# GpSimd's overflow steps dealt over seven turns of the expert loop, and a last stage whose first tile VectorE sums

## The reference, cut to what matters

```
order = jnp.argsort(e_flat)                  # tokens sorted by expert
xs = h2[slot_tok].reshape(n_blocks, MOE_BLOCK, d)
def expert_block(args):
    xb, e = args
    return (jax.nn.silu(xb @ w_gate[e]) * (xb @ w_up[e])) @ w_down[e]
ys = ys * slot_gate[:, None]
moe = jnp.zeros((n, d)).at[slot_tok].add(ys)
x = x + gt2 * moe
return rmsnorm(x, g_final)
```

## Time and profile before

| | us |
|---|---|
| median of 3 runs | 1537.36 |
| lowest, highest | 1535.84, 1541.0 |
| the profiled execution, its own time | 1537.67 |
| its span, first to last instruction | 1535.6 |
| TensorE busy in it | 1376.1 (90%) |
| VectorE busy | 931.7 (61%) |
| ScalarE busy | 679.1 (44%) |
| GpSimd busy | 283.9 (18%) |

### The profile page before, as it was taken

The page is one execution under the profiler, slowest core; times in us unless marked ns, Lnnn a source line. Parts: engine busy times, 40 slices in busy tenths (PEclk is TensorE's granted clock), DMA queues, the critical chain, the costliest instruction groups (busy, mean ns, idle before and its releaser), DMA issues. The chain is left out here.

```text
span 1535.6 us, 16837 instructions
## 1 busy us (share of the span) xinstructions
PE 1376.1 (90%) x6490; PEld 971.6 (63%) x6490; DVE 931.7 (61%) x1077; ACT 679.1 (44%) x772; POOL 283.9 (18%) x208
## 2 busy tenths in 40 slices
PE   1699999899999999989996647999999999999955
PEld 1555566456565665674554536888888888888832
DVE  8431230355555554654336564998898998988828
ACT  3500111123333332441111544877787878787713
POOL 0000010311111213210000693222222222222100
PEclk9899999899999999999997778999999999999968
DMA  9393235422222322343112574999999999999734
GB/s 358 103 305 113 68 108 168 134 61 79 70 82 70 88 74 66 92 143 124 69 55 83 189 300 147 382 395 382 383 369 392 379 390 382 388 381 385 270 147 200
DMA packets 101269, 321.47 MB, mean 209 GB/s; under 512 B 12140, under 2 KB 57284, under 8 KB 76613
## 3 DMA queue, kind: packets, MB, share of 16 engines
q1 hardware_dynamic: 89669, 296.25, 53.1%
q0 software_dynamic: 9216, 16.80, 2.9%
q10 hardware_dynamic: 2304, 7.34, 1.2%
HBM read 308.81 MB, written 28.31 MB: 220 GB/s over the span
## 5 line engine op out<-in xcount | busy, mean ns | idle before, releaser
L1630 DVE TENSOR_TENSOR w_low<-raw,w_high 128x2048 fp32r<-128x2048 f32 x128 | 291.7, 2300 | 38.6 <-ACT w_high L1570 36.0
L1570 ACT ACTIVATE w_high<-raw 128x2048 fp32r<-128x2048 f32 x128 | 240.9, 1908 | 15.8 <-PEq L981 15.8
L827 PE MATMUL p_j<-arena,raw 128*128 128x512 f32 (+1 forms) x448 | 184.3, 558 | 11.9 <-DVE raw L744 9.4
L1630 DVE TENSOR_TENSOR w_low<-arena,w_high 128x2048 fp32r<-128x2048 f32 x64 | 146.4, 2290 | 32.0 <-ACT w_high L1570 32.0
L827 PEld LDWEIGHTS p_j<-arena,raw 128*128 128x128 f32 x448 | 82.6, 192 | 86.4 <-issue 81.8
L1546 POOL DMA_INDIRECT y_rows<-arena,row x32 | 46.5, 1455 | 423.0 <-ACT arena L1591 422.7
L1570 ACT ACTIVATE w_high<-arena 128x2048 fp32r<-128x2048 f32 x64 | 122.3, 1912 | 3.3 <-DMA arena<-in_w_down 3.3
L449 PE MATMUL p_v<-wv,arena 128*128 128x384 f32 x320 | 105.5, 493 | 7.7 <-DMA wv<-in_w_in 7.7
L1504 PE MATMUL p_g<-w_high,x_high 128*128 128x512 f32 x256 | 103.6, 405 | 4.6 <-DVE x_low L1635 4.6
L1504 PE MATMUL p_y<-w_high,h_high 128*128 128x512 f32 x256 | 100.3, 392 | 3.4 <-issue 3.4
L761 DVE CUSTOM_DVE_ANT_0 prob<-p_s,table 128x640 f32<-128x640 f32 x96 | 75.2, 821 | 46.3 <-PE p_s L865 46.1
(11 more groups left out here) (286 smaller groups left out, 2504.9 us busy)
## 6 DMA issues: line engine op xcount, KB each, us to landing
raw<-in_w_gate SPq DMA_DIRECT2D x64, 1024.0 KB, 8.0
raw<-in_w_up SPq DMA_DIRECT2D x64, 1024.0 KB, 7.4
arena<-in_w_down SPq DMA_DIRECT2D x64, 1024.0 KB, 7.6
wa<-in_w_ada SPq DMA_DIRECT2D x24, 1024.0 KB, 6.4
table<-in_rpb SPq DMA_DIRECT2D x96, 192.0 KB
yy<-y_rows SPq DMA_DIRECT2D x8, 1024.0 KB, 12.7
raw<-in_w_in SPq DMA_DIRECT2D x12, 512.0 KB, 3.8
raw<-v_rows SPq DMA_DIRECT2D x96, 64.0 KB
```

What stands on the lines that cost most here:

```text
L827: last = pe.matmul(dst[:, 0:cols.stop - cols.start], wqk[:, k, w, :], s.ht[:, k, cols], start=(k == 0), stop=(k == KD - 1))
L1570: act.activation(x.high[i % SPLITS][:], x.raw[j][:, :], ACT.Copy).then_inc(high_ok, 1)
L1630: dve.tensor_tensor(x.low[i % SPLITS][:], x.raw[j][:, :], x.high[i % SPLITS][:], ALU.subtract).then_inc(low_ok, 1)
```

## The change

`build` is cut into seven methods with the same 80 steps in the same order: `count`, `add_up`, `owners`, `starts`, `turns`, `blocks`, `places`. They are called in turns 1 to 7 of GpSimd's loop, one each. In `finish`, tile 0 gets no diagonals and no TensorE products: VectorE makes two `scalar_tensor_tensor` and two adds. The `gain` row, its product and its copy go; ScalarE issues a DMA that reads `g_final` for all 128 partitions into `gains`.

```diff
@@ main_experts, gpsimd
+            steps = Counter(pool, over_ready)
             pool.wait_ge(c_in, 16)
             for n in range(NE):
                 if n + 2 < NE:
                     pool.wait_ge(x_turned, n + 1)
                     gather(pool, a, s, n + 2)
-                if n == 0:
-                    over.build(pool, Counter(pool, over_ready), s)
                 if n >= 1:
                     scatter(n - 1)
+                if n == 1:
+                    over.count(pool, steps)
+                if n == 2:
+                    over.add_up(pool, steps)
+                if n == 3:
+                    over.owners(pool, steps, s)
+                if n == 4:
+                    over.starts(pool, steps)
+                if n == 5:
+                    over.turns(pool, steps)
+                if n == 6:
+                    over.blocks(pool, steps)
+                if n == 7:
+                    over.places(pool, steps)
             scatter(NE - 1)
@@ finish, sync
-                sp.dma_start(gain[:], a.g_final).then_inc(g_in, 16)
                 for i in range(NT):
@@ finish, gpsimd
-                pool.memset(onerow[:], 1.0).then_inc(consts, 1)
                 pool.memset(epsb[:], EPS).then_inc(consts, 1)
@@ finish, tensor
-                pe.wait_ge(consts, 2)
-                pe.wait_ge(g_in, 16)
-                for h in range(2):
-                    last = pe.matmul(p_n[:, h, :], onerow[:], gain[:, h * 512:(h + 1) * 512], start=True, stop=True)
-                last.then_inc(spread, 1)
-                for i in range(NT):
+                for i in range(1, NT):
                     pe.wait_ge(y_in[i], 16)
-                    pe.wait_ge(diags, 2 * (i + 1))
-                    if i >= 2:
+                    pe.wait_ge(diags, 2 * i)
+                    if i >= 3:
                         pe.wait_ge(added, 2 * (i - 2) + 1)
@@ finish, scalar
-                act.wait_ge(spread, 2)
-                act.activation(halves(gains[:]), p_n[:], ACT.Copy).then_inc(spread_ok, 1)
-                act.wait_ge(consts, 2)
+                act.dma_start(gains[:], a.g_final.to_broadcast([P, D])).then_inc(g_in, 16)
+                act.wait_ge(consts, 1)
@@ finish, vector
+                def add_first():
+                    x1 = s.x1[:, 0, :]
+                    dve.wait_ge(y_in[0], 16)
+                    dve.wait_ge(spread_ok, 1)
+                    for k in range(2):
+                        c.step(dve.scalar_tensor_tensor(gated[k][:], yy[0][:, k, :], s.gates[:, k, 0:1], gate2[:], ALU.mult, ALU.mult))
+                    for k in range(2):
+                        dve.tensor_tensor(x1, x1, gated[k][:], ALU.add).then_inc(added, 1)
+                        dve.wait_ge(added, k + 1)
@@ scale(i)
                     if i == 0:
-                        dve.wait_ge(spread_ok, 2)
+                        dve.wait_ge(g_in, 16)
@@ order of VectorE
-                for i in range(NT):
+                for i in range(1, NT):
                     for k in range(2):
                         ...
                 for i in range(0, NT, 2):
-                    add(i)
+                    if i == 0:
+                        add_first()
+                    else:
+                        add(i)
                     add(i + 1)
```

More of the change, by code:

```diff
@@ L1402, in __init__, with halve, passed, count @@
         self.wide = free
-    def build(self, pool, c, s):
-        U, T = 2 * NT, N // CAP - 1
-        tt, ts = pool.tensor_tensor, pool.tensor_scalar
[L1410 to L1426, removed]
+    def halve(self, c, tt, dst, x, n):
+        while n > 2:
+            n //= 2
+            c.step(tt(x[:, :, 0:n], x[:, :, 0:n], x[:, :, n:2 * n], ALU.add))
+        c.step(tt(dst, x[:, :, 0], x[:, :, 1], ALU.add))
+    def passed(self, c, tt, ts, dst, x, n, compare):
+        flag = self.wide[:, 0:n]
+        c.step(ts(dst, x, float(CAP), None, compare))
+        for i in range(2, N // CAP):
+            c.step(ts(flag, x, float(CAP * i), None, compare))
+            c.step(tt(dst, dst, flag, ALU.add))
+    def count(self, pool, c):
+        tt, ts = pool.tensor_tensor, pool.tensor_scalar
+        self.passed(c, tt, ts, self.over, self.total, NE, ALU.is_gt)
+    def add_up(self, pool, c):
+        tt = pool.tensor_tensor
         now, other = self.sums
@@ L1433, in build, with owners @@
         c.step(tt(self.first, now, self.over, ALU.subtract))
+        self.upto, self.spent = now, other
+    def owners(self, pool, c, s):
+        tt, ts, now, other = pool.tensor_tensor, pool.tensor_scalar, self.upto, self.spent
         ends = self.wide[0:1, 0:OVB * NE].rearrange("p (b e) -> p b e", b=OVB)
@@ L1438, in build @@
         c.step(ts(ends, ends, 0.0, None, ALU.is_le))
-        halve(other[0:1, 0:OVB], ends, NE)
+        self.halve(c, tt, other[0:1, 0:OVB], ends, NE)
         c.step(ts(other[0:1, 0:OVB], other[0:1, 0:OVB], float(NE - 1), None, ALU.min))
@@ L1442, in build, with starts, turns, blocks @@
         c.step(pool.tensor_copy(s.blocks[:, OVB:OVB + 1], now[0:1, NE - 1:NE]))
+    def starts(self, pool, c):
+        U, tt = 2 * NT, pool.tensor_tensor
         pick = self.wide[:, 0:U * NE].rearrange("p (u e) -> p u e", u=U)
         c.step(tt(pick, self.one_e.rearrange("p (u e) -> p u e", u=U), self.first.unsqueeze(1).to_broadcast([P, U, NE]), ALU.mult))
-        halve(self.start, pick, NE)
-        passed(self.turn, self.rk, U, ALU.is_ge)
+        self.halve(c, tt, self.start, pick, NE)
+    def turns(self, pool, c):
+        U, tt, ts = 2 * NT, pool.tensor_tensor, pool.tensor_scalar
+        self.passed(c, tt, ts, self.turn, self.rk, U, ALU.is_ge)
         c.step(ts(self.rest, self.turn, -float(CAP), None, ALU.mult))
         c.step(tt(self.rest, self.rest, self.rk, ALU.add))
+    def blocks(self, pool, c):
+        U, tt, ts = 2 * NT, pool.tensor_tensor, pool.tensor_scalar
         c.step(tt(self.start, self.start, self.turn, ALU.add))
@@ L1461, in build, with places @@
             c.step(tt(self.code[:, :, d, :], hit, self.digits[:, U * d:U * (d + 1)].unsqueeze(2).to_broadcast([P, U, OVB]), ALU.mult))
+    def places(self, pool, c):
+        U, ts = 2 * NT, pool.tensor_scalar
         for u in range(U):
@@ L1853, in finish @@
         yy = [t.sb(f"yy{b}", [P, 2, D]) for b in range(NT)]
-        diag = t.sb("diag", [P, NT, 2, P])
+        diag = t.sb("diag", [P, NT - 1, 2, P])
         gated = [t.sb(f"gated{b}", [P, D]) for b in range(2)]
-        gain = t.sb("gain", [1, D])
         gains, gate2 = t.sb("gains", [P, D]), t.sb("gate2_rows", [P, D])
-        onerow, epsb = t.sb("onerow6", [1, P]), t.sb("epsb6", [P, 1])
+        epsb = t.sb("epsb6", [P, 1])
         ss, root, rstd, tmp = (t.sb(n, [P, NT]) for n in ("ss6", "root6", "rstd6", "tmp6"))
         p_s = [t.ps(f"p_s6{b}", [P, 2, 512]) for b in range(2)]
-        p_g, p_n = t.ps("p_g6", [P, 2, 512]), t.ps("p_n6", [P, 2, 512])
+        p_g = t.ps("p_g6", [P, 2, 512])
         y_in = [t.sem(f"y_in{b}") for b in range(NT)]
@@ L1902, in _ @@
                         for k in range(2):
-                            last = pe.matmul(p_s[i % 2][:, h, :], diag[:, i, k, :], yy[i][:, k, h * 512:(h + 1) * 512], start=(k == 0), stop=(k == 1))
+                            last = pe.matmul(p_s[i % 2][:, h, :], diag[:, i - 1, k, :], yy[i][:, k, h * 512:(h + 1) * 512], start=(k == 0), stop=(k == 1))
                     last.then_inc(gathered, 1)
@@ L1922, in _ @@
                 c = s.chain.on(dve)
+                def add_first():
[7 more added lines that the diff above has]
+                        dve.wait_ge(added, k + 1)
                 def add(i):
-                    dve.wait_ge(gathered, i + 1)
-                    if i == 0:
-                        dve.wait_ge(spread_ok, 1)
+                    dve.wait_ge(gathered, i)
                     x1, g = s.x1[:, i, :], gated[i % 2]
@@ L1942, in scale @@
                         dve.scalar_tensor_tensor(x1, x1, rstd[:, n:n + 1], gains[:], ALU.mult, ALU.mult).then_inc(scaled, 1)
-                for i in range(NT):
+                for i in range(1, NT):
                     for k in range(2):
-                        dve.tensor_scalar(diag[:, i, k, :], s.ident[:], s.gates[:, k, i:i + 1], None, ALU.mult).then_inc(diags, 1)
+                        dve.tensor_scalar(diag[:, i - 1, k, :], s.ident[:], s.gates[:, k, i:i + 1], None, ALU.mult).then_inc(diags, 1)
                 for i in range(0, NT, 2):
-                    add(i)
+                    if i == 0:
+                        add_first()
+                    else:
+                        add(i)
                     add(i + 1)
```

## The result

The changed kernel takes 1571.18 us (median of 4 runs, 1569.43 to 1574.87) against 1538.11 us, a ratio of 1.0217 (95% interval 1.0191 to 1.0243). That is 2.2% slower, 4 us above the forecast of 1567 and inside its range. The profiled execution took 1572.16 us, its span is 1570.2 us, 34.6 more than before.

What follows compares the result with a forecast made beforehand. TensorE was taken to bound the expert loop at 17.75 us a turn, with one 32.49 us hole. Removed stall -34.3, new waits +56.3, clock +8.4 and last stage -1.3 gave +29.1 us: forecast 1567 us, range 1552 to 1583.

Steps and rivals of the forecast that it cites:

- The removed stall: Expert loop: TensorE's wait for the gather of expert 3 goes, with its clock loss, -34.3 us.
- The order in GpSimd's list: Expert loop: each batch stands between a scatter and the next gather, making four TensorE waits, 56.3 us in sum.
- the short batches: Expert loop: add_up, starts and blocks cost nothing, as each runs during the stall in front of it.
- G: Expert loop: moment when TensorE has finished `gate_up(n, 1)` and wants `turn_x(n + 1)`; the next comes 17.75 us later.
- clock: After each of four stalls TensorE's clock must come back: 2.1 us each, 8.4 in all.
- The landing: Late gathers behind count, owners and turns land 8.0 us after they start; the one behind places takes 5.0.
- Two batches: Owners (10 steps) last until G + 22.6, gather at 23.4; turns (15 steps) until G + 21.5, gather at 22.3.
- On the port: Gather issue beside line 1630 taken as slow, 2.44 us against 1.14; by the skill's page the sum would be 3.9 lower.
- Delays TensorE almost one for one: Expert loop: whatever is put between a scatter and the gather behind it delays TensorE by nearly its own length.
- The 0.7 us between landing and need: Expert loop: a normal gather lands at G + 17.0 and is wanted at G + 17.75, taken as its slack.
- The last stage: `finish`: TensorE sums three tiles instead of four, so tile 3's sum is ready earlier: -1.3 us (-2.6 to +0.4).
- the sign that the fourth tile would start some 1 us earlier: Last stage: the fourth tile's line 1929 should start 1 us or so earlier, relative to the stage's start.

Runs made afterwards that it cites:

- split: Changed kernel, scatters one turn later, places dealt by four over turns 7 to 10; four last-stage variants: 1505.14, 1502.09, 1499.87 and 1499.98 us.
- later: Changed kernel with every scatter one turn later in GpSimd's list, same batches in the same turns: 1519.03 us, ratio 0.9886 to before.
- ahead: Changed kernel with each batch ahead of its turn's scatter instead of behind it: 1525.02 us, ratio 0.9940 to before.
- dose1: Kernel before, with one useless GpSimd step added between scatter and gather in each of turns 8 to 28: 1537.00 us, ratio 1.0003.
- dose4: Kernel before, with four useless GpSimd steps added between scatter and gather in each of turns 8 to 28: 1567.78 us, ratio 1.0192.
- fin_only: Kernel before with only the last stage (`finish`) of the change, overflow steps as before: 1538.04 us, ratio 1.0016.

## Why the prediction was right

**The removed stall** was predicted at 34.3 us and is gone: in the changed kernel turn 2 takes 17.74 us with no wait, and the four `split` kernels, in which nothing takes its place, come out 33 to 38 us faster. From the transposes of expert 2 to those of expert 31 their traces have 514.9 us each, the kernel before 549.3: 34.4 us.

**The order in GpSimd's list** was the right thing to read, and `later` and `ahead` show it. The holes stand where they were predicted, before experts 4, 6, 8 and 10, and the short batches were covered.

| before expert | batch | gather issued at G + | landing | wait | clock |
|---|---|---|---|---|---|
| 4 | count | 20.8, measured 20.8 | 8.0, 10.2 | 11.1, 13.1 | 2.1, 1.5 |
| 6 | owners | 23.4, 21.3 | 8.0, 9.0 | 13.6, 12.5 | 2.1, 2.3 |
| 8 | turns | 22.3, 20.6 | 8.0, 10.4 | 12.6, 13.1 | 2.1, 2.3 |
| 10 | places | 31.7, 31.5 | 5.0, 4.2 | 19.0, 17.9 | 2.1, 1.8 |

The first number is the predicted one. The waits sum to 56.5 against 56.3, the clock to 7.9 against 8.4. That the sum is this close is partly luck: two terms were off and cancel. **The landing was sized too small**, 8.0 where 9.0 to 10.4 was measured. I took the gather at 856 us (7.4) as the nearest row, but its issue of 2.29 us began before the weights flowed. From the end of the issue the three landings take 6.7 to 7.3 us; the rest is the issue itself, 2.4 to 3.0 us beside line 1630. **Two batches were sized too long**, owners by 2.1 and turns by 1.7 us: more steps found VectorE between line-1630 instructions than I had placed there (of the 15 of turns ten took 0.22 to 0.25 us). Places came out right (31.7, 31.5), though not every step there got through between two such instructions: one took 4.70 us and one 4.64, which is two of them in a row.

**On the port** the rows went against one sentence of the Trainium skill (SBUF — State Buffer, Who interferes with whom), by which descriptor writing is not held up by such a `tensor_tensor`; the section marks it as inferred. A gather's issue takes 2.29 to 3.04 us when it starts while line 1630 runs, and 0.99 to 1.24 otherwise, in the changed kernel, and `dose1` against `dose4` (1.12 and 3.21) shows that the moment decides: the held-up issue ends 0.9 to 1.0 us after the VectorE instruction that it met. With its other sentence, that the two exclude each other, the trace agrees: up to 2.34 us for a step of 0.25.

**"Delays TensorE almost one for one" was wrong for small batches.** The 0.7 us between landing and need is not the slack. The issue can go 2.4 us later for nothing, as `dose1` shows, and the cost then begins with a jump. For batches of 14 to 25 us it made no difference.

**The last stage** was predicted at -1.3 us (-2.6 to +0.4) and measured at +0.1, inside its bounds but no gain, so the sign that the fourth tile would start some 1 us earlier did not come. The term that was mis-sized is TensorE's tile 1: I had it start at 8.2 us after SyncE's first issue plus half a tile at most (1.4), and it started at 9.6, the late edge (tile 1 landed at 10.9 in `fin_only`), and then took nearly the full half-clock time, 6.5 us. In six traces with the new stage tile 1 landed 4.1 to 5.9 us behind tile 0, in six with the old one 2.6 to 4.0. The stretch from the first load's issue to the fourth tile is 22.6 to 24.0 us with the new one and 20.9 to 23.2 with the old.

Between the predicted +29.1 us and the 34.6 by which the spans differ there is no single cause: the last stage (1.4), the stages before the loop and its first two turns (1.0 each), two later turns that waited 0.6 us each for a gather, and some 1.2 us in turns of 17.84 to 17.90 us instead of 17.74; the waits (+0.2) and the clock (-0.5) nearly cancel. By the medians the change is +33.1 us.

## What to carry to other kernels

Before moving work into an in-order queue, ask what is queued behind it and when that is due: here a batch was moved out of one gather's way into those of four others, and the order of one line was worth 43 to 51 us. A transfer that lands just in time may still have room to be issued later, or none at all a microsecond on; a few added instructions per turn measure that edge. When steps share a port with a busy engine, count how many of that engine's instructions they will meet, and remember that curing the stall also takes away the idle time in which they run fast.

## What the runs showed of the hardware that I had not expected

- Two indirect DMAs in one queue: going 2.4 us later, the second lands at the same moment (12.8 and 12.7 us after the first one's start), mostly 3.5 to 3.9 us behind the landing of the first.
- A gather's issue that met a VectorE `tensor_tensor` with two SBUF inputs took up to 3.2 us, otherwise 1.0 to 1.2. GpSimd's small steps ran at their own pace (0.22 to 0.29 us) beside VectorE's `x_low` instruction of 1.22 us, which has one of its two inputs in PSUM (909.51 to 910.73 in the changed kernel).
- Useless transposes before the last stage's first product raised TensorE's clock in it from a mean of 0.80 to 1.00 and took 2.6 us off 24 instructions.
- A wait of TensorE of 12 to 18 us was followed by a turn 1.3 to 2.4 us longer, the one of 32.5 us by 1.6 and the one of 44.6 us by 2.7. After the waits of 2.1 to 2.9 us in `dose4` the turn was longer (19.5 us) three times out of ten, and after the one of 2.36 us in `ahead` too (19.45 us).
